# Two transformer blocks with 32 experts on one core: expert choice by a running maximum, a later residual product, and eight smaller loads into the second ring place

## The chip, the cores and the metric

One Trainium2 chip, one of its cores. The metric is the device time of one execution in microseconds (us). The median of three runs of the kernel before is 1616.52 us (1615.97 to 1616.59).

## What is computed

256 tokens of width 1024, float32 throughout. Two layers of a first block (gated feed-forward, a mixer of retention and latent attention, a second feed-forward) are followed by a second block: a mixer (grouped attention, a gated linear recurrence, an output projection), and then a mixture of experts. The change touches only the passage into the mixture and the choice of experts:

```python
# D = 1024, N_GROUPS = 4, EXPERTS_PER_GROUP = 8, TOP_K = 2, D_EXPERT = 512
g_prob = softmax(t @ w_rg + b_rg)                  # one group per token
p_g, g_idx = top_k(g_prob, 1)
e_logits = (t @ w_re + b_re).reshape(-1, 4, 8)
e_sel = e_logits of the chosen group
p_e, e_idx = top_k(softmax(e_sel), 2)              # two experts in it
p_e = p_e / sum(p_e)
for e in range(32):
    hid = silu(t @ w_gate[e]) * (t @ w_up[e])
    y = y + (hid * dense_w[:, e:e+1]) @ w_down[e]
```

`top_k` takes the lower index first where values are equal, so the kernel has to count equal ones.

## The kernel before

**Stages.** A plan of seven stages runs the dense layers. Their weights pass through `raw`, are split by ScalarE into a high part (`whi`, L832) and by VectorE into a low part (`wlo`, L1286), six 4 KB places each (`SLOTS`), and are used by TensorE in three products (L2106 to L2108). The last stage, `mix2`, ends with an output projection whose last two weight jobs (28 and 29, two halves each) are used first for token tile 0 and then for tile 1. After each half of tile 1 TensorE raises `split_used`; after the very last it raises `y_ready`. VectorE adds the result to `x` (L1364).

**The router** (`experts`, in the code of each engine). TensorE transposes `x` (L2666), ScalarE and VectorE copy it to `hcol` (L1216, L1923), TensorE multiplies it with `w_router` (L2677) and turns the logits (L2682). Then TensorE copies the four quarters of `x` into four PSUM banks by products with the identity (L2688, the holding products below); expert results are added there later. VectorE meanwhile chooses (L1950 to L1978): the group maxima, a count of equal values by a scan (a sum that restarts at each group), the first of them, the rest, the second maxima, another count. It ends in `both`, a 0/1 table of tokens by experts, which raises `picks_ready`. TensorE counts tokens by products with `both` (L2706 to L2710), runs one `keep_busy` product (L2113), gathers the tokens of the first block (`gather`, L2721), runs two more `keep_busy` products and starts the loop over experts. VectorE in between makes `take` (L1992), the table of block numbers `cum` (L1997), and turns the gathered rows into `h_e` (L2011, L2013).

**The experts.** Each expert has 4 MiB of gate and up weights (`expert_gu`) and 2 MiB of down weights (`expert_dn`), loaded from HBM by SP's DMA queue into a ring of three places; expert 3 lies in tiles of its own (`kept_gu`, `kept_dn`). The loop over an expert's blocks of 32 tokens is `block_of` (L2766 gate and up, L2786 down). Experts 0 to 3 are loaded ahead, in pieces, as the dense layers give memory free. Place 1 of the ring lies over `whi` and `wlo`: gate/up chunk 0 to 5 over `whi` places 0 to 5, chunks 6 and 7 over `wlo` places 0 and 1, down chunks 0 to 3 over `wlo` places 2 to 5. `kept_gu[2]` lies over `x` and `kept_gu[3]` over `hcol`.

**SP's queue** is in order: an issue whose wait is not met holds back all behind it. After the last weight of the dense layers it issues the rest of place 1 behind `y_ready`, `kept_gu[3]` behind the router's products and `kept_gu[2]` behind the holding products (`logits_done` 4), reads a number of `cum`, and then refills place 0 with expert 4: first half when TensorE has done half of expert 0's gate and up chunks (`gu_half_done`, L615), second half when it has done all (L617), down after L2786 (L629). From expert 7 on, one issue takes the whole gate and up part (L623).

## Time and profile before

| | us |
|---|---|
| median of three runs | 1616.52 |
| lowest, highest | 1615.97, 1616.59 |
| the profiled execution | 1615.38 |
| its span, first to last instruction | 1613.3 |
| TensorE busy in the span | 1480.5 |
| VectorE busy | 1014.5 |
| ScalarE busy | 702.1 |

The profile is of one execution. Its span is 2.1 us shorter than the time of the same execution, which has the start and the end around it. A row of the timeline gives the start, the duration, the engine, the source line, the operation and what it writes and reads; a number in square brackets is the engine's idle time before it, and what ended that. Matmuls are pipelined, so their rows overlap by a part. The granted clock is given as a share of 2.4 GHz. Transfers are asked for by SP and carried by 16 DMA engines; the DMA share is the mean busy share of these.

### The profile page before, as it was taken

What the parts mean: (1) busy time and instruction counts of PE and PEld (TensorE: products, weight loads), DVE (VectorE), ACT (ScalarE), POOL (GpSimd) and SP (SyncE); (2) the same over time, 40 slices, a digit from 0 to 9 for tenths busy, and PEclk for the clock granted to TensorE, in tenths of its full rate; (3) what the DMA queues carried; (4) which work ended last, traced back from release to release, by engine and by line L of the source; (5) the groups of instructions that cost most, each with busy time, mean ns of one, the idle gap of its engine ahead of it and who ended that gap; (6) DMA issues with size and microseconds to landing.
All of it is one profiled execution on the core that took longest, in us unless ns stands there. A gap on an engine that the chain in (4) does not pass through costs nothing.

```text
span 1613.3 us, 28471 instructions
## 1 busy us (share of the span) xinstructions
PE 1480.5 (92%) x10831; PEld 1158.8 (72%) x10832; DVE 1014.5 (63%) x1888; ACT 702.1 (44%) x1215; POOL 68.5 (4%) x88
## 2 busy tenths in 40 slices
PE   9999999999999999999999999999999776666666
PEld 7888888888888888888888889888854333233333
DVE  6777788677777777788677777988744321222122
ACT  6555566555555555666555556846320000000000
POOL 0000040000001000030200000001000000000000
PEclk9999999999999999999999999999999988888889
DMA  9665365365555655363465654353999999999997
GB/s 327 205 205 182 114 233 198 105 212 186 190 192 169 214 178 192 110 242 131 143 218 182 201 181 166 128 186 120 384 411 423 429 433 431 431 428 435 429 429 329
DMA packets 150093, 407.41 MB, mean 253 GB/s; under 512 B 5376, under 2 KB 98928, under 8 KB 139920
## 3 DMA queue, kind: packets, MB, share of 16 engines
q1 hardware_dynamic: 148800, 404.28, 67.6%
q0 software_dynamic: 1232, 2.29, 0.8%
q8 instruction: 41, 0.67, 0.2%
q14 instruction: 20, 0.16, 0.0%
HBM read 405.50 MB, written 1.05 MB: 252 GB/s over the span
## 4 chain that ended last, share of the span: by engine, by line
PE 74%; DMA 19%; DVE 4%; ACT 2%; issue 1%; SPq 0%; DVEq 0%; ACTq 0%
PE bank L2147 20%; DMA expert_gu<-in_exp_gu 18%; PE bank L2153 10%; PE bank L2106 10%; PE bank L2107 10%; PE bank L2108 10%; PE bank L2766 5%; DVE wlo L1286 1%; PE bank L2786 1%; PE bank L2696 1%; DMA raw<-in_ffn_w_up 1%; PE bank L2721 1%; PE bank L2479 0%; ACT whi L832 0%; DVE small L1431 0%
## 5 line engine op out<-in xcount | busy, mean ns | idle before, releaser
L1286 DVE TENSOR_TENSOR wlo<-raw,whi 128x1024 fp32r<-128x1024 f32 (+1 forms) x396 | 449.3, 1183 | 65.0 <-ACT whi L832 64.8
L832 ACT ACTIVATE whi<-raw 128x1024 fp32r<-128x1024 f32 (+1 forms) x396 | 382.7, 1021 | 69.7 <-PE bank L2108 68.2
L2147 PE MATMUL bank<-hboth,whi 128*128 128x512 f32 x1408 | 350.7, 392 | 1.9 <-DVE hboth L1329 1.3
L2147 PEld LDWEIGHTS bank<-hboth,whi 128*128 128x128 f32 x1408 | 258.6, 188 | 53.4 <-issue 2.0
L2766 PE MATMUL bank<-expert_gu,h_e 128*32 128x256 f32 x1984 | 155.4, 481 | 114.0 <-DMA expert_gu<-in_exp_gu 109.3
L2766 PEld LDWEIGHTS bank<-expert_gu,h_e 128*32 128x32 f32 x1984 | 76.9, 137 | 192.0 <-issue 171.5
L2153 PEld LDWEIGHTS bank<-hboth,wlo 128*128 128x128 f32 x1408 | 191.6, 191 | 13.4
L2153 PE MATMUL bank<-hboth,wlo 128*128 128x256 f32 x1408 | 195.8, 283 | 0.0
L2043 DVE SCALAR_TENSOR_TENSOR e_sg<-e_th,bank 128x128 f32<-128x128 f32 x33 | 9.5, 288 | 286.1 <-ACT e_th L1242 286.1
L2106 PE MATMUL bank<-whi,hboth 128*128 128x512 f32 (+2 forms) x384 | 150.5, 392 | 1.4 <-DVE hboth L1329 0.9
L2108 PE MATMUL bank<-whi,hboth 128*128 128x512 f32 (+2 forms) x384 | 147.1, 383 | 0.0
L2107 PE MATMUL bank<-wlo,hboth 128*128 128x512 f32 (+2 forms) x384 | 146.9, 383 | 0.0
L2106 PE MATMUL bank<-whi,act_hi 128*128 128x512 f32 x352 | 138.2, 393 | 0.0
L2107 PE MATMUL bank<-wlo,act_hi 128*128 128x512 f32 x352 | 138.2, 393 | 0.0
L2108 PE MATMUL bank<-whi,act_lo 128*128 128x512 f32 x352 | 137.2, 390 | 0.0
L1242 ACT ACTIVATE e_th<-bank 128x128 f32<-128x128 f32 x33 | 9.1, 277 | 265.4 <-PE bank L2766 265.1
L874 ACT ACTIVATE th<-gr 128x256 f32<-128x256 f32 x88 | 36.7, 418 | 131.8 <-DVE gr L1384 131.8
L2106 PEld LDWEIGHTS bank<-whi,hboth 128*128 128x128 f32 x384 | 72.3, 188 | 17.0 <-issue 3.1
L2108 PEld LDWEIGHTS bank<-whi,hboth 128*128 128x128 f32 x384 | 72.2, 188 | 13.6
L2107 PEld LDWEIGHTS bank<-wlo,hboth 128*128 128x128 f32 x384 | 72.3, 188 | 12.0
L879 ACT ACTIVATE act_hi<-act_f 128x256 fp32r<-128x256 f32 x88 | 36.8, 418 | 91.8 <-DVE act_f L1392 91.8
L2108 PEld LDWEIGHTS bank<-whi,act_lo 128*128 128x128 f32 x352 | 66.2, 188 | 14.4
(392 smaller groups left out, 1789.6 us busy)
## 6 DMA issues: line engine op xcount, KB each, us to landing
expert_gu<-in_exp_gu SPq DMA_DIRECT2D x24, 4096.0 KB, 38.1
expert_dn<-in_exp_dn SPq DMA_DIRECT2D x29, 2048.0 KB, 38.7
raw<-in_ffn_w_gate SPq DMA_DIRECT2D x44, 1024.0 KB, 5.5
raw<-in_ffn_w_up SPq DMA_DIRECT2D x44, 1024.0 KB, 7.4
raw<-in_ffn_w_down SPq DMA_DIRECT2D x44, 1024.0 KB, 4.9
raw<-in_w_in SPq DMA_DIRECT2D x36, 1024.0 KB, 5.2
expert_gu<-in_exp_gu SPq DMA_DIRECT2D x8, 2048.0 KB, 19.0
expert_gu<-in_exp_gu SPq DMA_DIRECT2D x10, 1024.0 KB, 6.8
```

Of the source, the lines that this page charges most:

```text
L832: nc.scalar.activation(slot_view(whi, slot, src), src, ACT.Copy).then_inc(hi_ready, inc)
L874: nc.scalar.activation(th[:, o % 2, :], gr[:, o % 2, :], ACT.Tanh, scale=0.5).then_inc(th_ready, 1)
L879: nc.scalar.activation(act_hi[:, o % 2, :], act_f[:, o % 2, :], ACT.Copy).then_inc(acthi_ready, 1)
L1286: nc.vector.tensor_tensor(slot_view(wlo, slot, src), src, slot_view(whi, slot, src).bitcast(F32), ALU.subtract).then_inc(lo_ready, inc)
L2106: nc.tensor.matmul(o, sh, mh, start=first, stop=False, skip_group_check=shared)
L2107: nc.tensor.matmul(o, sh, ml, start=False, stop=False, skip_group_check=shared)
L2108: return nc.tensor.matmul(o, sl, mh, start=False, stop=last, skip_group_check=shared)
L2147: nc.tensor.matmul(out_[:], wh[:, k, :], hboth[:, k, :, :], start=k == 0, stop=False, skip_group_check=True)
L2153: ins = nc.tensor.matmul(out_[:, 0:S], wl[:, k, :], hhi[:, k, :], start=False, stop=k == KC - 1, skip_group_check=True)
L2696: ins = nc.tensor.matmul(Y[2 * t + q_ // 2][:, (q_ % 2) * S:(q_ % 2 + 1) * S], give[rows_, t * P:(t + 1) * P], y_sb[rows_, :], start=False ...
L2721: ins = nc.tensor.matmul(bank[6][BS * q_:BS * (q_ + 1), 0:D // Q], take[:, t, :], xn[:, t, q_ * (D // Q):(q_ + 1) * (D // Q)], start=t == ...
L2766: ins = nc.tensor.matmul(bank[4][BS * q_:BS * (q_ + 1), 0:2 * P], h_e[:, c, :], gu(c, q_), start=c == 0, stop=c == KC - 1, tile_position=( ...
```

## The change

**Choice of experts.** A scan with add and max (`running`) over all 36 logits of a token tile gives a running maximum that restarts at each group, since `far` holds -1e30 where a group starts. Its last value in a group is the group's maximum. The second value of a group comes from `lower`, the smaller of running maximum and next logit, by one reduction. One scan (`nth`) then counts the values equal to the second; what lies above it is the first choice. The tables `hit` and `above` give `both`. The two tables `pick`, the group's exponent input (`g_less`) and the gap come behind `both`. Seven memsets stand at the head of the router's part of VectorE, three of them moved there from behind the choice.

**Holding products.** Three of the four stand where all four were; the fourth comes behind the gather, in the place of two `keep_busy` products. TensorE no longer waits for `expin_ready` ahead of the counts.

**Loads.** Place 1's 2 MiB of down and 2 MiB of gate/up weights that were issued as three transfers behind `y_ready` are now eight of 512 KiB: two behind the first half of job 28, two behind its second half, four behind `y_ready`. `kept_gu[2]` is loaded in two halves, the second behind the last holding product. TensorE waits for `consts_loaded` up to 14 transfers, not 9, ahead of the first expert.

```diff
+        running = at("running", [P, T, LOGITS], 121)
+        far = at("far", [P, T, LOGITS], 121.3125)
+        lower = at("lower", [P, T, NG, EG - 1], 121.625)
...
                 piece(jobs - 2)
                 piece(jobs - 1)
+                for half in range(2):
+                    sp.wait_ge(split_used, OPEN + mid_pos(last, jobs - 2, half) + 1)
+                    gate_up_part(1, 1, 3 + half, 4 + half, consts_loaded)
+                    down_part(1, 1, 1 + half, 2 + half, consts_loaded)
                 sp.wait_ge(y_ready, ends_of(last + 1))
-                gate_up_part(1, 1, 2, 4, gu_landed[1])
-                gate_up_part(1, 1, 4, 6, gu_rest_landed[1])
-                down_part(1, 1)
+                gate_up_part(1, 1, 2, 3, gu_landed[1])
+                gate_up_part(1, 1, 5, 6, gu_rest_landed[1])
+                down_part(1, 1, 0, 1, consts_loaded)
+                down_part(1, 1, 3, 4)
                 sp.wait_ge(logits_done, 2)
                 kept_part(3, kept_landed)
                 sp.wait_ge(squares_ready, 2 * (last + 1) + 2)
                 sp.wait_ge(xn_ready, T)
                 sp.wait_ge(logits_done, 4)
-                kept_part(2, kept_landed)
+                kept_part(2, kept_landed, 0, 1)
+                sp.wait_ge(logits_done, 5)
+                kept_part(2, kept_landed, 1, 2)
                 sp.wait_ge(cum_ready, 1)
...
                 n = turned(i)
+                V.memset(upto[:, :, 0:1], 0.0)
+                link(V.memset(far[:], 0.0))
+                link(V.memset(far[:, :, 0:1], -1e30),
+                     V.memset(far[:, :, NG:].rearrange("p t (g e) -> p t g e", g=NG)[:, :, :, 0:1], -1e30))
+                V.memset(blocks[:, 2, :], ROUNDER)
+                V.memset(fcum[:, 0:1], 0.0)
+                V.memset(cum[:, 0:1].bitcast(F32), 0.0)
...
+                done(step(V.tensor_tensor_scan(flat(running[:]), flat(far[:]), flat(logits[:]), 0.0, ALU.add, ALU.max)))
+                e_low = step(V.tensor_tensor(lower[:], re[:, :, :, 0:EG - 1], le[:, :, :, 1:EG], ALU.min))
+                g_upto = step(V.tensor_tensor(upto[:, :, 1:NG + 1], running[:, :, 0:NG], g_max, ALU.is_equal))
+                done(e_low)
+                e_max = step(V.tensor_reduce(m2, lower[:], AX, ALU.max))
+                done(g_upto)
+                step(V.tensor_tensor(g_first, upto[:, :, 1:NG + 1], upto[:, :, 0:NG], ALU.subtract))
...
-                for t in range(T):
-                    for h in range(2):
-                        ins = nc.tensor.matmul(Y[2 * t + h][:], ident[:], x[:, t, h * 512:(h + 1) * 512], start=True, stop=False,
-                                               skip_group_check=True)
-                ins.then_inc(logits_done, 1)
+                hold(0, 0)
+                hold(0, 1).then_inc(logits_done, 1)
+                hold(1, 0)
...
-                pe.wait_ge(expin_ready, 1)
                 pe.wait_ge(picks_ready, 1)
...
                 gather()
-                keep_busy(bank[4][:, 0:S], ident[:], square[:], 2)
-                pe.wait_ge(consts_loaded, 32 + 16 * 9)
+                hold(1, 1).then_inc(logits_done, 1)
+                pe.wait_ge(consts_loaded, 32 + 16 * 14)
```

**SP's queue before**, from the last weights of the dense layers to the router (`expert_gu_176` and `expert_dn_179` are place 1, 175 and 178 place 0, `kept_gu_183` is `kept_gu[2]`, `kept_gu_184` is `kept_gu[3]`):

```order
L642 DMA expert_dn_178<-in_exp_dn 128x2048 [waits lo_ready] x2
L658 DMA expert_gu_176<-in_exp_gu 128x2048 [waits y_ready]
L658 DMA expert_gu_176<-in_exp_gu 128x2048
L648 DMA expert_dn_179<-in_exp_dn 128x4096
L653 DMA kept_gu_184<-in_exp_gu 128x2048 [waits logits_done]
L653 DMA kept_gu_183<-in_exp_gu 128x2048 [waits logits_done,xn_ready,squares_ready]
L701 TENSOR_LOAD cum [waits cum_ready]
L701 ISA x2
L615 DMA expert_gu_175<-in_exp_gu 128x4096 [waits gu_half_done]
```

and with the change:

```order
L645 DMA expert_dn_178<-in_exp_dn 128x2048 [waits lo_ready] x2
L661 DMA expert_gu_176<-in_exp_gu 128x1024 [waits split_used]
L650 DMA expert_dn_179<-in_exp_dn 128x1024
L661 DMA expert_gu_176<-in_exp_gu 128x1024 [waits split_used]
L650 DMA expert_dn_179<-in_exp_dn 128x1024
L661 DMA expert_gu_176<-in_exp_gu 128x1024 [waits y_ready]
L661 DMA expert_gu_176<-in_exp_gu 128x1024
L650 DMA expert_dn_179<-in_exp_dn 128x1024 x2
L656 DMA kept_gu_184<-in_exp_gu 128x2048 [waits logits_done]
L656 DMA kept_gu_183<-in_exp_gu 128x1024 [waits logits_done,xn_ready,squares_ready]
L656 DMA kept_gu_183<-in_exp_gu 128x1024 [waits logits_done]
L711 TENSOR_LOAD cum [waits cum_ready]
```

Four issues stand ahead of the wait for `y_ready` that stood behind it, each of half the width or less, and an issue with a wait for the last holding product stands ahead of the reading of `cum`.

**TensorE before**, from the holding products to the first expert (L2113 is `keep_busy`, L2721 the gather):

```order
L2688 MATMUL bank<-x,ident 128x512 x4
L2706 MATMUL bank<-both,square 128x32 [waits picks_ready,expin_ready]
L2707 MATMUL bank<-both,square 128x32
L2708 MATMUL bank<-both,square 128x32
L2709 MATMUL bank<-both,square 128x32
L2710 MATMUL bank<-both,square 128x32
L2113 MATMUL bank<-square,ident 128x256
L2721 MATMUL bank<-xn,take 32x256 [waits xn_ready,take_ready]
L2721 MATMUL bank<-xn,take 32x256 x7
L2113 MATMUL bank<-square,ident 128x256 x2
L2799 TENSOR_LOAD cum [waits cum_ready,consts_loaded]
L2799 ISA x2
```

and with the change (L2698 holds, L2733 gathers, L2123 is `keep_busy`):

```order
L2698 MATMUL bank<-x,ident 128x512 x3
L2718 MATMUL bank<-both,square 128x32 [waits picks_ready]
L2719 MATMUL bank<-both,square 128x32
L2720 MATMUL bank<-both,square 128x32
L2721 MATMUL bank<-both,square 128x32
L2722 MATMUL bank<-both,square 128x32
L2123 MATMUL bank<-square,ident 128x256
L2733 MATMUL bank<-xn,take 32x256 [waits xn_ready,take_ready]
L2733 MATMUL bank<-xn,take 32x256 x7
L2698 MATMUL bank<-x,ident 128x512
L2811 TENSOR_LOAD cum [waits cum_ready,consts_loaded]
```

One holding product went from ahead of the counts to behind the gather, and two `keep_busy` products are gone.

**VectorE before**, the last twelve instructions of the choice and what follows it (a scan is listed as SCALAR_TENSOR_TENSOR):

```order
L1965 SCALAR_TENSOR_TENSOR rest<-first,logits 128x64 [waits dve_step]
L1966 TENSOR_TENSOR gs<-logits,one 128x8
L1968 TENSOR_REDUCE gs<-rest 128x8 [waits dve_step]
L1970 TENSOR_TENSOR pick<-first,gs 128x2x32
L1972 TENSOR_TENSOR hit_195<-rest,gs 128x64 [waits dve_step]
L1974 SCALAR_TENSOR_TENSOR nth_197<-route,hit_195 128x64 [waits dve_step]
L1975 TENSOR_TENSOR hit_in<-hit_195,gs 128x64
L1977 SCALAR_TENSOR_TENSOR pick<-nth_197,hit_in 128x2x32 [waits dve_step]
L1978 TENSOR_TENSOR both<-pick 128x64 [waits dve_step]
L1979 TENSOR_TENSOR gs<-gs 128x8
L1980 TENSOR_TENSOR gs<-gs 128x8 [waits dve_step]
L1981 TENSOR_REDUCE one<-gs 128x2 [waits dve_step]
```

and with the change, from the reduction to the second value on:

```order
L1970 TENSOR_REDUCE gs<-lower 128x8 [waits dve_step]
L1972 TENSOR_TENSOR gs<-upto 128x8 [waits dve_step]
L1974 TENSOR_TENSOR hit<-logits,gs 128x64 [waits dve_step]
L1975 TENSOR_TENSOR gs<-running,gs 128x8
L1976 TENSOR_TENSOR above<-logits,gs 128x64
L1978 SCALAR_TENSOR_TENSOR nth<-route,hit 128x64 [waits dve_step]
L1980 SCALAR_TENSOR_TENSOR gs<-gs 128x8 [waits dve_step]
L1982 TENSOR_TENSOR above<-above,gs 128x64 [waits dve_step]
L1984 TENSOR_TENSOR most<-hit,gs 128x64 [waits dve_step]
L1985 SCALAR_TENSOR_TENSOR hit<-nth,most 128x64 [waits dve_step]
L1986 TENSOR_TENSOR both<-hit,above 128x64 [waits dve_step]
```

Up to `both` there are 18 instructions before and 14 with the change.

## Rows read from the trace of the kernel before

**Rows 1.** The page: its span, and DMA's busy share in 40 slices.

```profile
span 1613.3 us, 28471 instructions
...
DMA  9665365365555655363465654353999999999997
```

**Rows 2.** Chain that ended last, experts stage: start us, us, what.

```profile
1282.94 38.04 DMA expert_gu<-in_exp_gu
1321.11 5.39 PE bank L2766 x64
```

**Rows 3.** Timeline of SP's queue around the router: start us, us, issue.

```profile
1173.82 0.80 SPq L658 DMA_DIRECT2D expert_gu<-in_exp_gu  x2
1174.67 0.43 SPq L648 DMA_DIRECT2D expert_dn<-in_exp_dn  x1
1177.60 5.08 SPq L653 DMA_DIRECT2D kept_gu<-in_exp_gu  x2
...
1188.36 0.33 SPq L615 DMA_DIRECT2D expert_gu<-in_exp_gu  x1
```

**Rows 4.** Windows: stretch, length, engines, TensorE clock granted, DMA share, GB/s.

```profile
1148.00:1156.00 8.00, 8.00 (x39) 6.66 (x38) 6.68 (x9) 4.01 (x5) 0.00 (x0) 1.00 0.97 390
1163.00:1174.00 11.00, 11.00 (x52) 9.12 (x51) 4.24 (x8) 2.21 (x3) 0.00 (x0) 1.00 1.00 420
1174.00:1176.00 2.00, 2.00 (x25) 1.83 (x24) 1.38 (x3) 1.73 (x3) 0.00 (x0) 1.00 0.96 299
1176.00:1190.00 14.00, 12.88 (x133) 7.33 (x129) 9.83 (x52) 4.71 (x12) 0.72 (x1) 1.00 1.01 425
1190.00:1194.00 4.00, 3.22 (x26) 1.16 (x26) 0.00 (x0) 1.27 (x3) 0.00 (x0) 1.00 0.92 344
1215.00:1600.00 385.00, 270.68 (x3760) 131.78 (x3752) 100.79 (x290) 19.15 (x58) 0.00 (x0) 0.86 1.00 430
```

**Rows 5.** DMA issues at 1174.67, 1182.3 and 1188.36, each asked alone: us to landing.

```profile
expert_dn<-in_exp_dn SPq DMA_DIRECT2D x1, 2048.0 KB, 11.4
...
kept_gu<-in_exp_gu SPq DMA_DIRECT2D x1, 1024.0 KB, 10.0
...
expert_gu<-in_exp_gu SPq DMA_DIRECT2D x1, 2048.0 KB, 9.3
```

**Rows 6.** Timeline of VectorE: last x updates, a copy behind them, memsets.

```profile
1171.11 0.69 DVE L1364 SCALAR_TENSOR_TENSOR x<-bank,x 128x512 f32<-128x512 f32 x1 [2.03 <-PE bank L2108]
...
1175.14 1.29 DVE L1923 COPY hcol<-bank 128x512 f32<-128x512 f32 x2 [0.62 <-PE bank L2666]
...
1182.44 0.09 DVE L1983 MEMSET blocks<- 128x32 f32 x1
```

**Rows 7.** Timeline of VectorE: the choice of experts.

```profile
1179.20 0.22 DVE L1950 TENSOR_REDUCE gs<-logits 128x8 f32<-128x64 f32 x1
1179.34 0.15 DVE L1951 TENSOR_REDUCE one<-logits 128x2 f32<-128x8 f32 x1
1179.45 0.23 DVE L1953 TENSOR_TENSOR hit<-logits,gs 128x64 f32<-128x64 f32 x1
...
1179.71 0.29 DVE L1957 TENSOR_TENSOR_SCAN nth<-route,hit 128x64 f32<-128x64 f32 x1
...
1181.78 0.23 DVE L1978 TENSOR_TENSOR both<-pick 128x64 f32<-128x64 f32 x1
```

**Rows 8.** Timeline of TensorE: from the holding products to the first expert.

```profile
1178.56 3.70 PE L2688 MATMUL bank<-x,ident 128*128 128x512 f32 x8
1182.15 0.38 PE L2706 MATMUL bank<-both,square 128*128 128x32 f32 x2
...
1183.87 1.07 PE L2721 MATMUL bank<-xn,take 128*32 128x256 f32 x16
1184.87 1.13 PE L2113 MATMUL bank<-square,ident 128*128 128x256 f32 x4
1186.37 3.66 PE L2766 MATMUL bank<-expert_gu,h_e 128*32 128x256 f32 x64 [0.36 <-issue]
```

88 lines of the change are left out of this document (39 added, 49 removed).

## The prediction

> **What bounds the kernel now.** I read the page first, for where an engine is the bound, then the chain that ended last, then windows around the place the change touches, then the timelines of SP, VectorE and TensorE there. In the page's 40 slices the DMA share is 9 in every slice of the last quarter but the one of the end [rows 1]; a slice is 40.3 us. The chain from 1250 us on repeats one pair of steps, of which one stands in the rows: some 38 us of waiting for `expert_gu`, then one group of gate and up products [rows 2]. So in the experts' stage the end is set by the stream of expert weights, and not by TensorE. The windows say when this begins: 420 GB/s with a share of 1.00 from 1163 to 1174, 425 from 1176 to 1190, and 430 from 1215 to 1600 [rows 4]. The stream is already full 20 us before expert 0 starts. In the router it has two shallow dips: 299 GB/s from 1174 to 1176, 344 from 1190 to 1194 [rows 4]. Everything this change does lies between 1169 and 1188 us, beside that stream. An engine that becomes faster here gives time only as far as a dip closes.
>
> What the dips are worth, at 430 GB/s: (430 - 299) x 2 / 430 = 0.61 us, and (430 - 344) x 4 / 430 = 0.80 us. Together 1.41 us. That is the ceiling of the whole change, 0.09% of the time. A measurement of this kernel tells about 0.2% from no change, 3.2 us.
>
> **The choice of experts.** The first reduction starts at 1179.20 and `both` at 1181.78, ending at 1182.01 [rows 7]. In these rows an instruction that waits for the one ahead starts 0.03 us after its end (0.22 + 0.03: 1179.20 to 1179.45), one that doesn't wait starts 0.11 to 0.14 after the start of the one ahead; after a scan I take 0.21, from 0.29 with the same overlap [rows 7]. I lay out the 14 new instructions with these: scan at 0 (0.30 long), `lower` 0.33, `upto` 0.47, reduction 0.60, `g_first` 0.74, `hit` 0.86, `tie` 1.00, `above` 1.12, count 1.26, `six` 1.47, `above` times group 1.61, `most` 1.75, the comparison 2.02, `both` 2.29. Before it was 1181.78 - 1179.20 = 2.58. So `both` comes 0.3 us sooner. What moved behind `both` (five instructions and `pick`) lies in the time in which TensorE counts. The seven memsets: the copy of `hcol` waits 0.62 us for the transposes with VectorE idle [rows 6]; a memset of 32 columns takes 0.09 [rows 6], so with two waits they take some 0.4 us, and that idle time covers them. Without this cover the copy, and with it the router, would come up to 0.4 us later.
>
> **The holding products.** They run from 1178.56 for 3.70 us, 0.925 each, to 1182.26, and the first counting product starts at 1182.15 [rows 8], so before the change a sooner `both` would have gained about nothing: TensorE was as late as VectorE. With three, TensorE is free at 1181.34 and waits for `both` instead, so the 0.3 us pass on: counts at 1181.85, gather at 1183.57. Behind the gather `keep_busy` of 1.13 us is replaced by one holding product of 0.925, and the first expert product follows its end after 0.37 (1184.87 + 1.13 = 1186.00; 1186.37) [rows 8]. New start: 1184.87 - 0.3 + 0.925 + 0.37 = 1185.87, **0.5 us sooner**. Bounds: 0.3 (if `h_e` sets it, which moves only with the gather) and 0.5. New idle time of TensorE is 0.5 us before the counts. The clock was granted in full in every window up to 1194 [rows 4], which hold an idle time of 0.8 us and more (12.88 busy of 14, 3.22 of 4), so I cost it at nothing.
>
> SP issues the refill of place 0 at 1188.36 [rows 3], when half of expert 0's gate and up group is done (1186.37 + 3.66 / 2 = 1188.20). It moves with expert 0 to **1187.86**. The second half of `kept_gu[2]` is now ahead of it in SP's queue, behind the last holding product (about 1185.5), with the reading of `cum` behind it. TensorE's own reading takes at most the 0.37 us above, so SP is ready by about 1186.3 and nothing is held back.
>
> **The loads.** Place 1's last 4 MiB are issued at 1173.82 to 1175.1 now [rows 3]. VectorE's update at 1171.11 follows job 28 of token tile 1, and such a pair of halves takes 2.03 + 0.69 = 2.72 us [rows 6], so the two halves are done near 1169.7 and 1171.0. Two MiB are then issued 3 to 4 us earlier, and the queue does not run empty at 1174: the first dip closes, 0.61 us. Nothing new is moved: all of it is the same bytes.
>
> Against this stands the size. Eight transfers of 512 KiB and two for `kept_gu[2]` carry 5.24 MB. The only stretch of the trace in which pieces of 512 KiB take a good share is 1148 to 1156, at 390 GB/s, against 420 in the stretch of 1 MiB pieces [rows 4]. At 390 instead of 420 the 5.24 MB take 13.4 instead of 12.5 us, 0.96 us more. The other bound is nothing, since 390 is a mixture with other causes. I take the middle, 0.5 us. The Trainium skill speaks against such loads (DMA: Bandwidth & Descriptors, section Rules for kernel authors): at least 1 MiB per DMA for bandwidth; its section Bandwidth lists 341 GB/s for a lone transfer of 1 MB and 425 for 16 MB. With 341 for these bytes one would estimate 15.4 us and a loss of 2.9; this trace's 1 MiB pieces move at 420 in a full queue [rows 4], so it agrees on the direction at most.
>
> **The sum.** Two limits hold at the second dip. By bytes: 0.61 + 0.80 - 0.5 = 0.9 us sooner. By issue: the refill starts 0.5 us sooner, and the stream behind it has no gap to give. The smaller one counts: 0.5 us. From there to the end the stream is full, so the end moves by as much. Profiled execution: 1615.38 - 0.5 = 1614.9, span 1612.8. The median of the runs is 1.14 above that execution, so the forecast is 1616.52 - 0.5 = **1616.0 us**.
>
> **The rivals.**
>
> *The gain moves from one dip to the other.* The first dip closes, the pieces cost what they may cost (0.96), the second opens wider, since its bytes are exhausted sooner. For it: the end of the queue's work does not depend on how its middle is packed. Against it: the refill's issue does move with expert 0. Time 1616.5, within 0.2 us. Chance 0.27.
>
> *Both dips close.* The queue never runs empty and the pieces cost nothing. For it: the refill's transfer lands 9.3 us after its issue, where 2 MiB at 430 take 4.9 [rows 5], so work was queued ahead of it. Time 1616.52 - 1.41 = 1615.1. Chance 0.15.
>
> *Slower: the small pieces, and expert 0 waiting for one of them.* TensorE now waits for `consts_loaded` 14 before expert 0, which includes down chunk 0 of place 1, third of the four issued after 1173.8. Today's 2 MiB down transfer lands at 1174.67 + 11.4 = 1186.07 [rows 5]. The new last piece would land there less 0.61 for the closed dip and plus eight pieces' loss (4.19 MB, 0.77), at 1186.2, and the third a piece (1.25 us) sooner, at 1185.0; expert 0 would start at 1185.87, its reading of `cum` at 1185.5. The margin is 0.5 us. It decides from where the pieces move slower than 375 GB/s, or land out of turn. At 350 GB/s the 5.24 MB cost 15.0 - 12.5 = 2.5 us: more than both dips, 1616.52 + 2.5 - 1.41 = 1617.6. By the skill's figure of 341 it would be 1618.0. Against it: a share of 0.97 at 390 was the lowest in a loaded stretch. Chance 0.13.
>
> *Slower by the clock.* If the clock were halved after TensorE's new idle time, a group of 64 products would take what it takes at 1321 us, 5.39 instead of 3.66 [rows 2, 8]. The refill would be issued up to 1.7 us later, 1617.7; through experts 1 and 2, with their down parts held back as well, over 3 us. Against it is the full clock before 1194. Chance 0.05.
>
> *The forecast* has 0.40. The range goes from 1614.6 (both dips closed, and the runs' own spread of 0.5 below) to 1617.6, the slower rival. Only the worst end of the clock case is over 0.2% slower, and no case known to me over 0.2% faster, since the dips hold 1.41 us; I leave 0.03 and 0.02 for what the profile doesn't show, and 0.95 for no change.
>
> **What would show it.** Right: `both` starts 2.3 us after the scan and not 2.6; the counting product starts after an idle time ended by VectorE; the first expert product near 1185.9 and the refill's issue near 1187.9; the window 1174 to 1176 at 420 GB/s or so; a second dip still there near 1190 with some of its depth; the same 38 us of waiting for `expert_gu` later. Wrong: TensorE idle before expert 0 behind a DMA (the slower rival); no dip at 1190 (both closed); a stretch of 1170 to 1188 below 400 GB/s (the size costs more); or an end that moves by more than 1.5 us either way, which would mean that something else than the stream's dips sets it.

## The result and the profile after

| | before | after |
|---|---|---|
| median | 1616.36 us (1614.25 to 1617.61, 22 runs) | 1617.95 us (1615.12 to 1621.21, 22 runs) |
| ratio | 1 | 1.0012 [1.0007, 1.0018] |
| profiled execution | 1615.38 us, span 1613.3 | 1615.42 us, span 1613.3 |

The change costs 1.6 us by the medians, 0.07 to 0.18% by the interval. The forecast was 1616.0 us, 0.5 sooner, with a range up to 1617.6. The measured median, 1617.95, lies outside it, on the side of the slower rival that was given 0.13. The two profiled executions don't show the loss: they are equally long. What the profile of one execution can show is where each predicted step landed. The loss itself lies in how far the executions of the new kernel scatter upwards, and more profiles were needed to see it.

The page, span and DMA share as in [rows 1]:

```profile
span 1613.3 us, 28473 instructions
...
DMA  9665365365555655373465654353999999999997
```

VectorE's timeline (start us, us, what), the head of the router and the choice, against [rows 6, 7]:

```profile
1174.51 0.06 DVE L1929 MEMSET upto<- 128x2 f32 x1
...
1175.17 1.29 DVE L1938 COPY hcol<-bank 128x512 f32<-128x512 f32 x2 [0.20 <-PE bank L2676]
...
1179.23 0.31 DVE L1966 TENSOR_TENSOR_SCAN running<-far,logits 128x72 f32<-128x72 f32 x1
...
1181.33 0.23 DVE L1986 TENSOR_TENSOR both<-hit,above 128x64 f32<-128x64 f32 x1
...
1183.65 0.18 DVE L2007 CAST cum<-fcum 128x32 int32<-128x32 f32 x1
```

The memsets lie in the idle time of the copy, which shrinks from 0.62 to 0.20 us. `both` starts 2.10 us after the scan where 2.29 was laid out and 2.58 was measured before. TensorE's timeline of the same stretch, against [rows 8]:

```profile
1178.59 2.84 PE L2698 MATMUL bank<-x,ident 128*128 128x512 f32 x6
1181.61 0.41 PE L2718 MATMUL bank<-both,square 128*128 128x32 f32 x2 [0.18 <-DVE both L1986]
...
1183.36 1.07 PE L2733 MATMUL bank<-xn,take 128*32 128x256 f32 x16
1184.36 1.13 PE L2698 MATMUL bank<-x,ident 128*128 128x512 f32 x2
1186.46 3.66 PE L2778 MATMUL bank<-expert_gu,h_e 128*32 128x256 f32 x64 [0.98 <-issue]
```

Counts, gather and the last holding product all come 0.5 us sooner, the last row but one at 1184.36 against 1184.87. Then the gain is gone: the first expert product starts at 1186.46, 0.09 later than before. Behind the holding product TensorE is idle for 0.98 us, and the profile names no engine that it waited for. SP's queue, against [rows 3]:

```profile
1169.77 0.33 SPq L661 DMA_DIRECT2D expert_gu<-in_exp_gu  x1
1171.13 0.33 SPq L661 DMA_DIRECT2D expert_gu<-in_exp_gu  x1
1174.70 0.91 SPq L650 DMA_DIRECT2D expert_dn<-in_exp_dn  x2
1177.63 8.21 SPq L656 DMA_DIRECT2D kept_gu<-in_exp_gu  x3
1188.45 0.33 SPq L618 DMA_DIRECT2D expert_gu<-in_exp_gu  x1
```

The early pieces go out at 1169.77 and 1171.13, as forecast. The refill of place 0 is issued at 1188.45 and not at 1187.86. The windows (stretch, length, engines, TensorE clock granted, DMA share, GB/s) against [rows 4]:

```profile
1174.00:1176.00 2.00, 2.00 (x25) 1.83 (x25) 1.65 (x10) 1.70 (x3) 0.00 (x0) 1.00 1.00 410
1176.00:1190.00 14.00, 12.09 (x130) 6.55 (x124) 9.68 (x49) 4.74 (x12) 0.72 (x1) 1.00 1.05 415
1190.00:1194.00 4.00, 3.22 (x24) 1.20 (x24) 0.00 (x0) 1.19 (x2) 0.00 (x0) 1.00 0.96 400
1169.00:1190.00 21.00, 19.09 (x172) 12.51 (x170) 12.27 (x60) 7.59 (x16) 0.72 (x1) 1.00 1.03 417
1215.00:1600.00 385.00, 271.14 (x3760) 132.15 (x3748) 100.72 (x290) 19.14 (x58) 0.00 (x0) 0.87 1.00 429
```

The first dip is closed (410 against 299 GB/s), the second is shallower (400 against 344). So in this execution the stream is ahead at 1194, and yet the end is where it was.

### The profile page after: what moved, and what is told of

The parts are those of the page before. It is cut to its first block, busy times and chain, and to the rows that moved or that the text cites. A ratio compares the mean times of both kernels' runs of the same rounds, so it can differ in the third digit from the quotient of the medians.

```text
span 1613.3 us, 28473 instructions
## 1 busy us (share of the span) xinstructions
PE 1480.6 (92%) x10827; PEld 1158.4 (72%) x10828; DVE 1014.6 (63%) x1892; ACT 702.2 (44%) x1215; POOL 67.5 (4%) x88
## 3 DMA queue, kind: packets, MB, share of 16 engines
q0 software_dynamic: 1232, 2.29, 0.7%
## 4 chain that ended last, share of the span: by engine, by line
PE 73%; DMA 18%; DVE 5%; ACT 2%; issue 1%; POOL 0%; DVEq 0%; SPq 0%; ACTq 0%; POOLq 0%
PE bank L2157 20%; DMA expert_gu<-in_exp_gu 18%; PE bank L2163 10%; PE bank L2116 10%; PE bank L2117 10%; PE bank L2118 10%; PE bank L2778 5%; DVE wlo L1296 2%; PE bank L2798 1%; PE bank L2709 1%; PE bank L2733 1%; ACT hboth L850 1%; ACT whi L842 0%; PE bank L2489 0%; DVE small L1441 0%
```

## What held expert 0

Expert 0 begins with two readings of the table `cum` into TensorE's registers. They stand behind two waits, one for `cum_ready`, one for `consts_loaded`. Before, `cum` is complete here:

```profile
1184.17 0.19 DVE L1997 CAST cum<-fcum 128x32 int32<-128x32 f32 x1
```

It ends at 1184.36, and the first product starts at 1186.37, 2.01 us later. So two readings and the loop's set-up would take 2.0 us, and they ran beside the gather and `keep_busy`. After, `cum` is complete at 1183.83, 0.53 sooner, which alone would give 1185.84: the forecast's 1185.87. But there the readings have to wait for the 14th transfer as well. This is its issue (down chunk 0 of place 1, issued at 1174.70; KB, us to landing):

```profile
expert_dn<-in_exp_dn SPq DMA_DIRECT2D x1, 512.0 KB, 9.9
```

It lands at 1184.6, and 1184.6 to 1186.46 is 1.86 us. The transfer ended last, by 0.8 us. That is the theory with which the experiments began (theory A in the expectations): the wait for a late small piece, ahead of readings that take 2 us, eats the gain. Its rivals: the pieces or the early loads disturb the stream (theory B); the choice, the holding products or the clock (theory C); something later in the experts' stage gives the gain back.

## The experiments

All edits are to the changed kernel where nothing else is said. "Distance" is the time from the first holding product to the first expert product in the profiled execution: 7.81 us before, 7.87 after. It leaves out how early the router began in that execution.

**The wait, the loads and the choice apart.** Beside these, before had 1616.52 us in 33 runs.

`e1_after_again` is the changed kernel once more.

> The changed kernel again, unaltered, for a second profile beside the first. Theory A (expert 0's start sets the end: TensorE waits for the 14th counted transfer before expert 0, and the refill for expert 7, issued near 1234 us behind TensorE's chain through experts 0 to 4, finds the queue nearly dry, so the end moves with expert 0): slower than before by 1 to 2.5 us in the median; in an execution with a time t above the first profile's 1615.4 the first expert product starts later than 1186.46 by about as much. Theory B (small pieces): slower by the same, with expert 0 at 1186.5 in every profile and the loss in the stretch 1169 to 1190 us as GB/s. Theory C (the choice and the holding products cost it): the same loss, with the counting products or the clock late.

Measured: 1617.27 us (1615.56 to 1619.11), ratio 1.0003 [0.9994, 1.0012]. By itself this interval doesn't tell the kernel from before. The landing is at 1184.9 and the first product at 1186.67, again 1.8 behind it; distance 8.40.

`e2_own_sem` counts the five added transfers of place 1 on a semaphore of their own, so that only expert 1 waits for them:

```diff
-                    gate_up_part(1, 1, 3 + half, 4 + half, consts_loaded)
-                    down_part(1, 1, 1 + half, 2 + half, consts_loaded)
+                    gate_up_part(1, 1, 3 + half, 4 + half, last_landed)
+                    down_part(1, 1, 1 + half, 2 + half, last_landed)
...
-                pe.wait_ge(consts_loaded, 32 + 16 * 14)
+                pe.wait_ge(consts_loaded, 32 + 16 * 9)
...
                 for j in range(RING):
+                    if j == 1:
+                        pe.wait_ge(last_landed, 16 * 5)
                     expert(j, (j, 1), first=j == 0)
```

> The changed kernel, but the five added transfers of place 1 are counted on another semaphore that TensorE waits for ahead of expert 1; ahead of expert 0 it waits for the 9 transfers of before. Theory A: the first expert product starts at about 1185.8 (1.9 us behind the table of blocks at 1183.8) and the time falls by 2 us or more against the changed kernel, to 0.3 to 0.6 us under before; its spread falls to that of before. Theory B (small pieces): unchanged, 1 to 2.5 us slower than before. Theory C: unchanged as well.

(The last wait on `last_landed` rises by the same five.) Measured: 1615.7 us (1614.33 to 1616.78), 0.9993 [0.9984, 1.0002]; distance 7.18.

`e3_loads_only` is the kernel before with the eight loads and the wait for 14, and nothing else:

```diff
+                for half in range(2):
+                    sp.wait_ge(split_used, OPEN + mid_pos(last, jobs - 2, half) + 1)
+                    gate_up_part(1, 1, 3 + half, 4 + half, consts_loaded)
+                    down_part(1, 1, 1 + half, 2 + half, consts_loaded)
...
-                pe.wait_ge(consts_loaded, 32 + 16 * 9)
+                pe.wait_ge(consts_loaded, 32 + 16 * 14)
```

> The kernel before with the eight loads of 512 KiB into place 1 and the wait for 14 transfers, the choice, the holding products and the last kept part as before. Theory A: the first expert product at 1186.5 or later, time 0.5 to 2.5 us over before. Theory B: 1 to 2.5 us over before, with the first expert product at 1186.4. Theory C: within 0.5 us of before.

Measured: 1616.78 us (1615.33 to 1621.04), 1.0007 [0.9998, 1.0016]; two of its eleven executions took 1621 us. Landing 1185.3, first product 1187.17, distance 8.24.

`e4_choice_hold` is the changed kernel with place 1's last 4 MiB in three transfers behind `y_ready`, as before, and the wait for 9:

```diff
-                gate_up_part(1, 1, 2, 3, gu_landed[1])
-                gate_up_part(1, 1, 5, 6, gu_rest_landed[1])
-                down_part(1, 1, 0, 1, consts_loaded)
-                down_part(1, 1, 3, 4)
+                gate_up_part(1, 1, 2, 4, gu_landed[1])
+                gate_up_part(1, 1, 4, 6, gu_rest_landed[1])
+                down_part(1, 1)
...
-                pe.wait_ge(consts_loaded, 32 + 16 * 14)
+                pe.wait_ge(consts_loaded, 32 + 16 * 9)
```

> The changed kernel with place 1 loaded in three transfers behind y_ready as before (the choice, the three holding products and the two halves of the last kept part stay). Theory A: the table of blocks is ready 0.5 us sooner, the first expert product starts near 1185.8, the refill for expert 7 near 1233.5, and the time is 0.3 to 0.6 us under before. Theory B: within 0.5 us of before, a little over for the two half pieces. Theory C: 1 to 2.5 us over before.

Measured: 1614.78 us (1613.08 to 1616.36), 0.9988 [0.9979, 0.9997]; distance 7.24. What follows: of these four, the two in which expert 0 doesn't wait for the 14th transfer have a distance of 7.2 and medians below before; the two with that wait are over 8.2, with medians above it. The intervals of three of the four reach 1, so the distances say more here than the times. The same eight loads, counted elsewhere, cost nothing that shows.

**The thin spot in the stream.** Comparing windows of the two traces further on, the stream of the changed kernel thins out at 1234 (before, then after):

```profile
1234.00:1242.00 8.00, 7.54 (x128) 3.78 (x124) 3.48 (x10) 0.53 (x2) 0.00 (x0) 1.00 1.02 416
```

```profile
1234.00:1242.00 8.00, 7.43 (x128) 3.94 (x128) 3.48 (x10) 0.66 (x2) 0.00 (x0) 1.00 0.92 360
```

There expert 7's gate and up weights go out in one transfer of 4 MiB, at 1234.03 before and here after, when TensorE has used up place 0:

```profile
1234.19 0.35 SPq L626 DMA_DIRECT2D expert_gu<-in_exp_gu  x1
```

The idea was that a stream that is ahead of TensorE has less queued at that moment, so that what it gained earlier is lost here. Three kernels load it in two halves, the first when half of the place is free:

```diff
-                with sp.Fori(1, NE // RING - 1) as r:
+                for j in range(RING):
+                    used = sp.value_load(cum[0:1, RING + KEPT - 1 + j:RING + KEPT + j], min_val=1, max_val=MAXB)
+                    (gate_up if j == 0 else gate_up_whole)(RING + KEPT + 1 + j, j, used)
+                    down(RING + KEPT + 1 + j, j, used)
+                with sp.Fori(2, NE // RING - 1) as r:
```

> The changed kernel, with the refill for expert 7 issued in two halves like those for experts 4 to 6 (first half when half of expert 4's gate and up chunks is done), the first loop round of experts 4 to 9 written out. Theory A (the queue runs dry near 1236 us because this refill is issued behind TensorE's chain): the dip of 1234 to 1242 us (360 and 346 GB/s in the two profiles of the changed kernel) closes, the time falls by 1 to 2 us against the changed kernel. Theory B (the pieces themselves cost the time, and the stream is full from there on): no change against the changed kernel. Writing out six experts could cost code loading; then slower by any amount with the chain's gaps longer.

> Both mends: the five added transfers awaited ahead of expert 1, and the refill for expert 7 in two halves. Theory A: 1 us or more under the changed kernel with its own semaphore alone, 1.5 to 2.5 us under before, the sum of both dips that the loads close. Theory B: as the own semaphore alone, 0.8 us under before.

> The choice, the three holding products, the loads of before, and the refill for expert 7 in two halves. Theory A: the window 1234 to 1242 was 410 GB/s with the loads of before, so there is little to close: 0 to 0.5 us under the same kernel with a whole refill, 1.5 to 2.2 us under before. Theory B: the same as with a whole refill.

Measured, beside before at 1616.25: on the changed kernel 1616.14 us (1615.19 to 1619.6), 1.0006 [0.9997, 1.0015]; with the own semaphore 1615.69, 0.9995 [0.9986, 1.0004]; on `e4` 1615.79 (1614.79 to 1618.13), 1.0 [0.9991, 1.0009]. In `e5` the window fills:

```profile
1234.00:1242.00 8.00, 7.63 (x128) 3.96 (x128) 3.48 (x10) 0.66 (x2) 0.00 (x0) 1.00 1.01 422
```

Its median is 1.5 us below the changed kernel's over all runs (1617.64), but three of its eleven executions took over 1618 us, and the other two kernels are no faster than without the halves. So the thin spot is real, it takes part in the loss at most, and mending it doesn't beat mending the wait. That it comes from a stream that is ahead isn't shown: the five profiles of the changed kernel have 342 to 375 GB/s there, and the lowest is that of `e14` (below), whose stream had lost time before.

**How much a late expert 0 costs.** `e8_delay` and `e9_delay16` put 4 and 16 more `keep_busy` products ahead of the wait:

```diff
                 hold(1, 1).then_inc(logits_done, 1)
+                keep_busy(bank[4][:, 0:S], ident[:], square[:], 4)
```

> The changed kernel with four more keep_busy products (2.26 us at 1.13 for two) between the last holding product and expert 0. TensorE is then free at 1187.75, and the first expert product starts near 1188.1, 1.65 us later than 1186.46. Theory A (the end moves with expert 0): 1.4 to 1.9 us slower than the changed kernel. Theory B (the end is set by the bytes alone): within 0.5 us of the changed kernel.

> The changed kernel with sixteen more keep_busy products behind the last holding product (four took 1.89 us), so that the first expert product starts near 1193, 6.6 us later than in the changed kernel. Theory A, as it stood (the end moves with expert 0, one for one): 6 to 7 us slower than the changed kernel. Theory A with slack (the run with four more moved expert 0 by 1.0 us and the time by 0.2 to 0.6): the first microsecond is nearly free, 5 to 6 us slower. Theory B (the bytes alone set the end): under 1 us.

Measured, beside before at 1616.29: `e8` 1617.83 us (1614.78 to 1618.49), 1.0008 [0.9999, 1.0017]; `e9` 1621.89 (1619.81 to 1623.98), 1.0035 [1.0023, 1.0047]. TensorE's timeline of the two, `e8` first:

```profile
1187.49 2.80 PE L2779 MATMUL bank<-expert_gu,h_e 128*32 128x256 f32 x48 [0.15 <-issue]
```

```profile
1192.78 3.66 PE L2779 MATMUL bank<-expert_gu,h_e 128*32 128x256 f32 x64
```

In `e8` the start of expert 0 is not the work of the four products. They and the transfer that is awaited (issued at 1174.83) stand so:

```profile
1185.44 1.89 PE L2123 MATMUL bank<-square,ident 128*128 128x256 f32 x8
```

```profile
expert_dn<-in_exp_dn SPq DMA_DIRECT2D x1, 512.0 KB, 10.8
```

The products end at 1187.33; the transfer lands at 1185.6, and the first product follows it after 1.9 us, as in the changed kernel. So `e8` delays only the executions whose transfer lands sooner than this one, and in the others it fills TensorE's idle time with work (0.15 us are left). Its distance, 8.78, is that of a middling execution of the changed kernel (7.87, 8.40, 8.59, 9.01 and 10.00 in five profiles), and its median is that of the changed kernel, 1617.83 against 1617.64. That is why the 1.4 to 1.9 us that theory A had expected of it did not come.

In `e9` the products do set the start. Its distance is 13.73, 5.9 us more than before's, and its time is 5.6 us over before's. Against the kernel with its own semaphore (7.2 us and 1615.46) it is 6.5 us of distance and 6.4 us of time. So a delay of expert 0 passes on nearly in full, in the median, and a difference in distance of 0.6 us is worth about 0.6 us.

`e10_own_again` and `e11_choice_hold_again` repeat `e2` and `e4`; `e12_choice_only` is the kernel before with the new choice alone, its loads and the four holding products as they were.

```diff
-                for t in range(T):
-                    for h in range(2):
-                        ins = nc.tensor.matmul(Y[2 * t + h][:], ident[:], x[:, t, h * 512:(h + 1) * 512], start=True, stop=False,
...
+                hold(0, 0)
+                hold(0, 1)
+                hold(1, 0)
+                hold(1, 1).then_inc(logits_done, 1)
...
-                pe.wait_ge(expin_ready, 1)
                 pe.wait_ge(picks_ready, 1)
```

> The changed kernel with the five added transfers awaited ahead of expert 1, once more. Theory A: 1 us or more under the changed kernel (1617.3 to 1618.0), 0.3 to 1.2 us under before, with its slowest execution under 1617.5. If the 1615.7 of the first time was chance: within 0.7 us of the changed kernel.

> The choice and the holding products with the loads of before, once more. Theory A: 0.5 us under before (expert 0 starts 0.5 us sooner). The 1.74 us of the first time are more than it explains: either they come down to 0.5 to 1 us here, or an earlier expert 0 gives more than its own shift. Theory B puts it level with the kernel with its own semaphore plus the cost of the small pieces, so 0.5 to 1.5 us under that.

> Only the choice of experts and its memsets: four holding products ahead of the counts, two keep_busy products behind the gather, the last kept part whole, the loads of before. The prediction's step says that TensorE was as late as VectorE: the first counting product can start only 0.03 us or so sooner, so expert 0 starts at 1186.3 and the time stays within 0.3 us of before. If the choice alone brings the gain, it is 0.5 us or more under before.

Measured: `e10` 1614.78 us (1614.28 to 1616.61), 0.9993 [0.9984, 1.0002]; `e11` 1616.18 (1613.67 to 1616.82), 0.9997 [0.9988, 1.0006]; `e12` 1615.79 (1613.89 to 1617.66), 0.9994 [0.9985, 1.0003]. The 1.7 us of `e4` did not repeat, so they are no result; the gain of the own semaphore did. TensorE in `e10`, then in `e12`:

```profile
1178.48 2.84 PE L2698 MATMUL bank<-x,ident 128*128 128x512 f32 x6
...
1184.24 1.12 PE L2698 MATMUL bank<-x,ident 128*128 128x512 f32 x2
1185.69 3.66 PE L2778 MATMUL bank<-expert_gu,h_e 128*32 128x256 f32 x64 [0.32 <-issue]
```

```profile
1178.89 3.70 PE L2691 MATMUL bank<-x,ident 128*128 128x512 f32 x8
...
1186.50 3.66 PE L2772 MATMUL bank<-expert_gu,h_e 128*32 128x256 f32 x64 [0.30 <-issue]
```

In `e10` the distance is 7.21 and the idle time 0.32, close to what the forecast had (1185.87 for the first product is a distance of 7.31, and 0.37 for the idle time). In `e12` it is 7.61, only 0.2 under before: with all four holding products ahead of the counts, TensorE is as late as `both`. Its median is 0.5 us under before, with an interval that holds no change, so how much of the 0.8 us of the own semaphore is the choice's alone isn't settled by the times.

**The wait kept, its place moved.** `e13_wait_behind` leaves all transfers and the wait for 14 as they are, and puts it behind the two readings:

```diff
-                pe.wait_ge(consts_loaded, 32 + 16 * 14)
...
                     hi = pe.value_load(cum[0:1, bass.ds(e + 1, 1)], min_val=1, max_val=MAXB)
+                    if first:
+                        pe.wait_ge(consts_loaded, 32 + 16 * 14)
                     with pe.Fori(lo, hi) as k:
```

> The changed kernel with the same wait for 14 transfers, but placed behind the two readings of the block table and not ahead of them. Theory A1 (the wait costs because the reading, some 1.8 us, begins only when the 14th transfer has landed at 1184.7): the reading now overlaps the landing, the first expert product starts near 1185.9 and the time is that of the kernel with its own semaphore, 1614.8 to 1615.7, 1 to 2 us under the changed kernel. Theory A2 (in the slower executions the 14th transfer lands some microseconds later than in the profiled ones, and that delay is the cost): half or less of it comes back, and the slowest executions stay above 1618. Theory B: no change.

Measured, beside before at 1616.47: 1615.57 us (1614.27 to 1617.29), 0.9995 [0.9986, 1.0004]. TensorE:

```profile
1179.04 2.84 PE L2698 MATMUL bank<-x,ident 128*128 128x512 f32 x6
...
1186.18 3.66 PE L2777 MATMUL bank<-expert_gu,h_e 128*32 128x256 f32 x64 [0.25 <-issue]
```

Distance 7.14. This is the cleanest of the tests, because not a byte or a transfer differs: the reading is beside the transfer instead of behind it, and the distance falls by 0.7 us and more against every profile of the changed kernel. The transfer landed early in this execution, at 1185.0; with the wait ahead of the readings the product would have come 1.8 us behind it, at 1186.8, and it came at 1186.18. Ahead of the readings the landing is an obstacle; behind them it is one only where it comes later than they end. All profiles but those of `e9` and `e18` together:

| profiles | distance | first product behind the 14th landing | behind the completion of `cum` |
|---|---|---|---|
| wait ahead of the readings (after, `e1`, `e3`, `e5`, `e8`, `e14` to `e16`) | 7.87 to 10.00 us | 1.8 to 1.9 us | 2.5 to 4.8 us |
| wait behind them (`e13`) | 7.14 | 1.2 | 1.9 |
| own semaphore (`e2`, `e6`, `e10`, `e17`) | 7.18 to 7.21 | -0.6 to 0.5 | 1.9 to 2.0 |
| old loads, new choice and holding products (`e4`, `e7`, `e11`) | 7.20 to 7.24 | not awaited | 1.9 to 2.0 |
| before, `e12` | 7.81, 7.61 | not awaited | 2.0 |

`e14`, `e15` and `e16` are the changed kernel, profiled once more each, to see its slower executions from inside.

> The changed kernel, one more profile. A1: first expert product 1.8 us behind the landing of the 14th transfer, 7.8 to 8.5 us behind the first holding product, whatever the time is. A2: in an execution above 1617.5 it lies 9 us or more behind.

> The same as the look before it: A1 7.8 to 8.5 us from the first holding product to the first expert product in any execution, A2 9 us or more in a slow one.

> The same once more: A1 7.8 to 8.5 us, A2 9 us or more in a slow execution.

They took 1617.37, 1619.41 and 1617.57 us, with distances of 10.00, 9.01 and 8.59. The 14th transfer in `e15` (issued at 1174.38) and `e14` (at 1174.89):

```profile
expert_dn<-in_exp_dn SPq DMA_DIRECT2D x1, 512.0 KB, 11.1
```

```profile
expert_dn<-in_exp_dn SPq DMA_DIRECT2D x1, 512.0 KB, 12.0
```

The same 512 KiB land after 9.9, 11.1 and 12.0 us in three executions of one kernel: near 1184.6, 1185.5 and 1186.9. TensorE's timeline in `e15`, and then two windows of it (the first of TensorE alone: length, busy, clock granted, DMA share, GB/s; the second with all engines):

```profile
1184.03 1.13 PE L2698 MATMUL bank<-x,ident 128*128 128x512 f32 x2
1187.27 5.27 PE L2778 MATMUL bank<-expert_gu,h_e 128*32 128x256 f32 x64 [2.12 <-issue]
```

```profile
1188.00:1190.00 2.00, 2.00 (x24) 0.50 0.93 373
...
1190.00:1194.00 4.00, 3.59 (x46) 1.38 (x38) 0.00 (x0) 0.37 (x1) 0.00 (x0) 0.93 0.63 202
```

and in `e14`, with the refill that it issues:

```profile
1188.77 5.35 PE L2778 MATMUL bank<-expert_gu,h_e 128*32 128x256 f32 x64 [3.11 <-issue]
```

```profile
1191.18 0.33 SPq L618 DMA_DIRECT2D expert_gu<-in_exp_gu  x1
```

Here both slower rivals of the prediction act in one chain. The piece lands late; TensorE is idle for 2.12 and 3.11 us; then the first group of 64 takes 5.27 and 5.35 us instead of 3.66. The clock granted during it is 0.50 in `e15` (1188 to 1190), which is 1.2 of 2.4 GHz, and 0.53 in `e14` (1190 to 1192). With that, place 0's refill is issued at 1190.88 in `e15` and at 1191.18 in `e14`, not at 1188.45, and from 1190 to 1194 the stream falls to 202 and 203 GB/s where it had 400. That is 4 x (400 - 202) / 429 = 1.8 us of stream; the two executions took 3.1 and 1.1 us more than the median of before. After idle times of 0.98, 1.51 and 1.70 us (after, `e1`, `e16`) the clock stayed full. `e16` reached a distance of 8.59 with full clock and still took 1617.57, so the landing alone costs something as well. `e8` says the same: with the idle time filled its median is no lower than the changed kernel's. What it lacks is the upper end: its highest execution is 1618.49, over which 9 of the 36 of the changed kernel lie. With 11 executions that is a hint that the clock makes the slowest ones, and no more.

A finer measure than the time is the landing of the weights for which TensorE waits at the last expert but one, near 1585: 1585.29 before; 1584.14, 1586.58, 1586.89, 1588.00 and 1588.35 in the changed kernel, at distances of 7.87, 8.40, 8.59, 10.00 and 9.01; 1585.86, 1583.98 and 1585.17 with the own semaphore. So by then the stream is late where expert 0 was late. How the loss divides between landing and clock in each execution stays open.

**A third repeat, and one reading less.** `e17_own_third` repeats the own semaphore, and `e18_own_one_read` takes away one of the two readings beside it, expert 0's loop starting at the constant 0:

```diff
-                    lo = pe.value_load(cum[0:1, bass.ds(e, 1)], min_val=0, max_val=MAXB)
+                    lo = 0 if first else pe.value_load(cum[0:1, bass.ds(e, 1)], min_val=0, max_val=MAXB)
```

> The changed kernel with the five added transfers awaited ahead of expert 1, a third time, for a version that beats both kernels. 0.5 to 1.5 us under before, no execution above 1617.6; if 1615.7 and 1614.8 were chance, level with before.

> The same, and expert 0's loop starts at the constant 0, so that one reading of the block table is left out ahead of it. If two readings in a row are what takes 1.8 to 2.0 us behind the table (1183.8 to 1185.8), the first expert product comes with the last holding product and h_e, near 1185.5, some 0.3 us sooner in distance from the first holding product (7.2 now), and the time is 0 to 0.3 us under the version with two readings. If a single reading takes as long, no change.

Measured, beside before at 1616.14: `e17` 1615.46 us (1614.26 to 1616.93), 0.9995 [0.9986, 1.0004]; `e18` 1614.06 (1613.28 to 1617.57), 0.9994 [0.9985, 1.0003]. TensorE in `e18`:

```profile
1178.93 2.84 PE L2698 MATMUL bank<-x,ident 128*128 128x512 f32 x6
...
1184.69 1.12 PE L2698 MATMUL bank<-x,ident 128*128 128x512 f32 x2
1185.79 3.66 PE L2778 MATMUL bank<-expert_gu,h_e 128*32 128x256 f32 x64
```

The distance is 6.86, and no idle time is left: the last holding product now ends last, so one reading less saves at least 0.34 us.

**All executions of one kernel together:**

| kernel | executions | median | highest |
|---|---|---|---|
| before | 153 | 1616.29 us | 1618.45 us |
| changed | 36 | 1617.64 us | 1621.21 us |
| own semaphore (`e2`, `e10`, `e17`) | 33 | 1615.46 us | 1616.93 us |
| choice and holding products, old loads (`e4`, `e11`) | 22 | 1615.40 us | 1616.82 us |

Of the 36 executions of the changed kernel 19 are above 1617.6 us, of the 33 with the own semaphore none. The version with the own semaphore is under before by 0.8 us and by a ratio of 0.9993, 0.9993 and 0.9995 in three measurements. Each interval by itself just holds 1; it is the threefold repeat that speaks for a gain, of 0.05 to 0.07%. It is the kernel to keep. `e18` has the lowest median, but from 11 runs that were not repeated, with a ratio of 0.9994.

## Why the prediction was wrong

*What bounds the kernel, and what the dips are worth.* Right in kind: the change moved the time by 1.6 us, and no version of it repeated a gain of more than 0.1%. But the dips were read from one execution, as if they were a property of the kernel. In `e12`, whose loads are those of before, the window 1174 to 1176 shows another depth than 299, and 1190 to 1194 none at all:

```profile
1174.00:1176.00 2.00, 2.00 (x21) 1.83 (x21) 1.49 (x9) 1.40 (x3) 0.00 (x0) 1.00 0.55 135
1190.00:1194.00 4.00, 3.22 (x24) 1.15 (x24) 0.00 (x0) 1.19 (x2) 0.00 (x0) 1.00 1.00 420
```

The eight loads brought nothing by themselves: with them (own semaphore, 1615.46) and without (`e4`, `e11`, 1615.40) the time is the same. That the issue of the refill counts, and not the bytes, fits this, since it moves with expert 0.

*The choice of experts, 0.3 us.* Right: 0.45 us by `both` (1181.78 to 1181.33), a little more than laid out, since instructions that don't wait overlap more than assumed.

*The holding products and "the first expert product follows its end after 0.37".* The step that failed. The 0.37 us were read as a fixed cost behind `keep_busy`. They are what is left over of two readings that start when `cum` is complete and take 2.0 us beside other work. That it is not `h_e` that ends last `e10` shows: `h_e` is complete there at 1185.30, 0.39 before the first product, and in `e18` 0.06 before it. As long as nothing else delays the readings, both views give the same number: 1185.84 by the readings, 1185.87 by the forecast, and the kernels without the wait reach a distance of 7.2 (after has 7.87) and 1615.5 us, 0.8 below before where 0.5 was forecast. The forecast describes these kernels, not this change. In the change the awaited transfer, which the sum had put at nothing, lands at 1184.6 to 1186.9, the first product follows 1.8 to 1.9 us behind it (1186.46 to 1188.77 where 1185.87 was forecast), and the median is 1.6 us above before instead of 0.5 below.

*The slower rival: expert 0 waiting for one of the pieces.* It had the right transfer and nearly the right landing (1185.0; measured 1184.6 to 1186.9). Its margin was wrong; it said "its reading of `cum` at 1185.5. The margin is 0.5 us". In the trace of before `cum` was complete at 1184.36, so in the changed kernel the readings could begin at 1183.83, and the landing forecast was not 0.5 us ahead of them but 1.2 behind. With the 1.9 us from landing to product, the prediction's own landing would have put the first product at 1185.0 + 1.9 = 1186.9 and made the rival the likeliest case. It also tied the danger to pieces slower than 375 GB/s or out of turn; from 1169 to 1190 the profiles with the pieces have 402 to 417.

*The size of the pieces, 0.5 us.* No loss shows, and none of this size is excluded: 0.5 us in 21 are 10 GB/s, and the profiles differ by more. (The 390 GB/s of 1148 to 1156, from which the term came, are 377 in the changed kernel's profile, though no transfer that early was changed.) In 1169 to 1190 the changed kernel moved 417 GB/s, and before had:

```profile
1169.00:1190.00 21.00, 19.88 (x177) 13.30 (x175) 12.15 (x56) 7.58 (x16) 0.72 (x1) 1.00 1.00 413
```

The Trainium skill's rule of at least 1 MiB per DMA (DMA: Bandwidth & Descriptors, Rules for kernel authors), beside which a loss of 2.9 us had been estimated, isn't borne out by this: in a queue that is full anyway the 512 KiB pieces went along at nearly the same rate, far above the 341 GB/s from which that loss was worked out.

*"From there to the end the stream is full, so the end moves by as much."* Not quite. The windows that were read for it jump from 1194 to 1215 and then average 385 us. In between, at 1234, the stream hangs on the issue of one 4 MiB transfer, and it thinned to 342 to 375 GB/s in the changed kernel. At the very end there is another loose link. TensorE in the last expert but one, before and then after:

```profile
1585.29 3.31 PE L2766 MATMUL bank<-expert_gu,h_e 128*32 128x256 f32 x32 [5.56 <-DMA expert_gu<-in_exp_gu]
...
1590.82 1.93 PE L2766 MATMUL bank<-expert_gu,h_e 128*32 128x256 f32 x32
```

```profile
1584.14 3.64 PE L2778 MATMUL bank<-expert_gu,h_e 128*32 128x256 f32 x32 [5.41 <-DMA expert_gu<-in_exp_gu]
...
1590.77 1.93 PE L2778 MATMUL bank<-expert_gu,h_e 128*32 128x256 f32 x32
```

The weights land 1.15 us sooner after, and the second half of the group starts at the same time. From the landing to the end the profiled executions took between 27.5 and 30.4 us, so a gain of the stream of 1 or 2 us can vanish in a single execution. This is why the two profiled spans are equal.

*The clock at nothing.* Right for three of the five profiled executions, wrong for two: the rival had the price (5.39 forecast, 5.27 and 5.35 measured) and took as its cause the new idle time before the counts, which is 0.18 us and harmless. The idle time after which the clock was halved is the one behind the last holding product, which the late landing makes.

*The chances.* The 0.95 for "no change", within 0.2%, stands: the ratio's interval, 1.0007 to 1.0018, lies within it. The predicted time and range don't. The range ended at the time of the slower rival worked out for a single cause. In `e14` and `e15` two act in one chain: a late transfer makes the idle time, and the halved clock follows it.

## What to carry to other kernels

Before a wait is raised or moved, look at what stands behind it on the same engine and how long that takes; here two readings of a table, 2 us that had been hidden, were put behind a transfer that needs 10 to 12. Put such a wait behind the readings, or count the added transfers on a semaphore that only their user waits for. And read a distance of 0.37 us between two products as what remains of the longest chain, not as a cost: find what that chain starts from. Where a margin is under 1 us and hangs on the landing of one transfer, one profile isn't enough, because its landing moved by 2 us from execution to execution here.

## What the runs showed of the hardware

- Two table readings into TensorE's registers and the loop's set-up take 1.9 to 2.0 us from the completion of the table to the first product (before 2.01, `e10` 1.97), and 1.8 to 1.9 from the landing of a transfer waited for, in eight profiles. One reading less saved at least 0.34. The Trainium skill gives about 600 ns as the floor of one such load (DMA: Bandwidth & Descriptors, Latency and other measured facts). Of two in a row no row here shows the parts; the sum and the loop's start are over it.
- The clock granted to TensorE fell to half after idle times of 2.12 and 3.11 us behind the holding products and stayed full after 1.70 and less, with the same work ahead of them. The length of the idle time alone doesn't say it. At the last expert but one `e8` waited 3.93 us and then had the full clock (1.00 granted from 1585 to 1587):

```profile
1585.01 1.93 PE L2779 MATMUL bank<-expert_gu,h_e 128*32 128x256 f32 x32 [3.93 <-DMA expert_gu<-in_exp_gu]
```

In the trace of before the same 32 products took 3.31 us behind 5.56 us of idle time.

- The landing of one 512 KiB transfer behind a full queue moved between 9.9 and 12.0 us from issue, in executions of the same kernel. What sets it was not tried.
